# A decoder layer whose expert stage begins the loads of its gates from ScalarE instead of SyncE

## The reference

```python
def block(xb):                                   # 128 tokens, 1024 features
    q = (xb @ w_query).reshape(tb, 8, 2, 128)
    s = jnp.einsum('thpc,hpnc->thpn', q, sub_keys)
    top_s, top_i = lax.top_k(s, 16)
    ...                                          # 16 x 16 candidates a head, the best 16 are kept
    g = jax.nn.softmax(best_s, axis=-1)
    u = expert_u[idx]                            # idx: 8 heads x 16 of 16384 experts
    h = jax.nn.gelu(jnp.einsum('thkd,td->thk', u, xb), approximate=False)
    w = (g * h).astype(xb.dtype)
    return jnp.einsum('thk,thkd->td', w, expert_v[idx])
```

## Time and profile before

| | |
|---|---|
| time, median of 3 runs | 2946.75 us (2942.84 to 2950.31) |
| the profiled execution | 2942.5 us, of which the span in the profile is 2940.7 us |
| PE busy | 2642.6 us (90%) |
| DVE busy | 2408.1 us (82%) |
| ACT busy | 867.9 us (30%) |
| POOL busy | 1319.5 us (45%) |
| moved by DMA | 685.24 MB, 233 GB/s over the span |
| the expert phase | from about 1207 us to the end |

### The profile page before, as it was taken

How to read it: one execution, slowest core, us unless ns; L and a number is a source line. 1 busy time by engine, 2 the same in 40 slices (tenths; PEclk the granted TensorE clock), 3 DMA queues, 4 the chain that set the end, 5 groups by cost and what they waited for, 6 DMA issues and landing times. The chain is left out here.

```text
span 2940.7 us, 46951 instructions
## 1 busy us (share of the span) xinstructions
PE 2642.6 (90%) x17459; PEld 1721.0 (59%) x17459; DVE 2408.1 (82%) x4501; ACT 867.9 (30%) x1463; POOL 1319.5 (45%) x869
## 2 busy tenths in 40 slices
PE   8999888798867765699999999999999999999996
PEld 3566655458867764455555555555555555555552
DVE  3244555574999998489999999999999999999998
ACT  2333333211114555422222222222222222222223
POOL 2110000210014442046666666666677767766772
PEclk9999989799978885799999999999999999999998
DMA  4000010261002243789999999999999999999994
GB/s 155 23 15 15 15 72 15 88 250 51 1 1 115 114 163 150 287 293 354 359 351 357 364 347 361 362 353 368 324 339 347 346 344 348 332 354 339 340 337 170
DMA packets 262958, 685.24 MB, mean 233 GB/s; under 512 B 35624, under 2 KB 118184, under 8 KB 258352
## 3 DMA queue, kind: packets, MB, share of 16 engines
q0 software_dynamic: 110592, 402.70, 36.8%
q1 hardware_dynamic: 152240, 280.98, 27.4%
HBM read 624.89 MB, written 58.72 MB: 232 GB/s over the span
## 5 line engine op out<-in xcount | busy, mean ns | idle before, releaser
L1886 PE MATMUL h_psum<-early 128*128 128x384 bf16 (+1 forms) x6144 | 859.2, 300 | 23.4 <-issue 12.7
L1904 PE MATMUL o_psum<-v_split,w_split 128*128 128x512 bf16 x3840 | 856.7, 381 | 20.1 <-DVE wide L1745 20.0
L1886 PEld LDWEIGHTS h_psum<-early 128*128 128x128 bf16 x6144 | 602.6, 98 | 279.4 <-issue 26.6
L1904 PEld LDWEIGHTS o_psum<-v_split,w_split 128*128 128x128 bf16 x3840 | 375.5, 98 | 461.4 <-DVE wide L1745 25.3
L1701 POOL DMA_INDIRECT early<-v_blocks,pick_index x320 | 486.2, 1520 | 200.7 <-DVE wide L1757 119.1
L1701 POOL DMA_INDIRECT early<-u_rows,pick_index x320 | 426.4, 1333 | 329.5 <-DVE dots L1753 214.8
L1757 DVE SCALAR_TENSOR_TENSOR wide<-early,dots,wide 128x1024 f32<-128x1024 f32 x320 | 399.4, 1281 | 34.0 <-DMA early<-v_blocks,pick_index 33.3
L1753 DVE CUSTOM_DVE_ANT_0 early<-early,wide 128x1024 f32<-128x1024 f32 x320 | 380.7, 1220 | 25.5 <-DMA early<-u_rows,pick_index 24.6
L1648 ACT ACTIVATE w_split<-act_out 128x640 bf16<-128x640 f32 x128 | 94.3, 737 | 706.1 <-DVE act_out L1721 648.4
L1635 ACT ACTIVATE act_out<-h_psum 128x384 f32<-128x384 f32 (+1 forms) x256 | 97.2, 431 | 522.5 <-PE h_psum L1886 479.7
L1110 PE MATMUL r_t_psum<-rt_x_t,early 128*128 128x128 f32 (+1 forms) x1920 | 234.6, 283 | 0.0
(11 more groups left out here) (202 smaller groups left out, 2961.2 us busy)
## 6 DMA issues: line engine op xcount, KB each, us to landing
early<-u_blocks SPq DMA_DIRECT2D x128, 512.0 KB
early<-v_blocks SPq DMA_DIRECT2D x128, 512.0 KB
gates<-wide SPq DMA_DIRECT2D x20, 2048.0 KB, 6.3
gate<-gates SPq DMA_DIRECT2D x32, 1280.0 KB
early<-w_query SPq DMA_DIRECT2D x8, 1024.0 KB, 5.9
att_w_raw<-w_fox SPq DMA_DIRECT2D x4, 1536.0 KB, 7.0
early<-u_rows,pick_index POOLq DMA_INDIRECT x320
early<-v_blocks,pick_index POOLq DMA_INDIRECT x320
```

Of the source, the lines that this page charges most:

```text
L1886: mm = pe.matmul(h_psum[k][:, half, 0:width * P], u_split[:, k, part, c], xs[:, first:first + width, xpart, c, :], start=(c == 0 and part ...
L1904: mm = pe.matmul(o_psum[(DENSE * p + t) % 2][:, half * 512:half * 512 + 512], w_split[:, p, q, part, t * P:(t + 1) * P], v_split[:, p, q, ...
```

## The change

SP no longer waits for `w_done` and no longer begins the loads of the gates inside `refill`. ACT begins them, behind `split_w_hi` of the fourth block of a group. That call has already waited for `gated` of the same block, so the buffer has been read for the last time; no other wait is added. The loads of groups 0 and 1 stay with SP. The 30 transfers have the same source, target and size. They now belong to ACT's DMA queue, which nothing used before.

```diff
@@ refill, on SP
                         if not (end and j >= 2 * GROUP - 2):
                             sp.wait_ge(v_split_done, b + 1)
                             load_v(b + 2, j % 2)
-                        if j % GROUP == GROUP - 1 and not end:
-                            sp.wait_ge(w_done, b + 1)
-                            load_gate(2 * i + 2 + j // GROUP, j // GROUP)
@@ blocks_of, on ACT
                         split_w_hi(b, j)
+                        if j % GROUP == GROUP - 1 and not (isinstance(i, int) and i == last):
+                            g, p = 2 * i + 2 + j // GROUP, j // GROUP
+                            act.dma_start(gate[:, p], gates[:, :, bass.ds(g * GROUP, GROUP), :]).then_inc(gate_in[p], 16)
```

## The result

The changed kernel took 2974.88 us in the median, the kernel before 2946.94. These are medians of eight executions each; one of the eight of either kernel was disturbed (4622.56 and 8551.71 us) and is left out of the ratio, which goes by the means of the other seven, 2971.77 and 2946.43. The ratio is 1.0086, with a 95% interval of 1.0061 to 1.0111. The forecast was 2933. The profiled execution took 2975.9 us, 33.4 us more than that of before.

The account below looks back on a forecast made before the run. PE was taken to bound the early expert groups and DVE, waiting for gathers, the later ones. 2942.5 - 13.8 + 0 + 0 = 2928.7 us, 2932.9 against the median, forecast 2933; 8-in-10 range 2921 to 2952.

Parts of the forecast that it names:

- the early half: Expert phase, 12 groups from 1407.38 to 2032.95 us, mostly dot products with U rows; PE bounds it, no gain expected.
- the later one: Expert phase, 14 groups from 2032.95 to 2784.68 us, mostly additions of V rows; DVE bounds it at 53.70 us a group.
- the 22 given as the most that could be gained: Later 14 groups: at 1.57 us less a group PE bounds them too, so the gain stops at 22 us.
- PE's pace of 52.13 us a group: Group time in the 12 early groups, where PE is always busy; taken as the floor for the later groups.
- ACT's 30 loads: Gate loads newly issued by ACT: up to 7 us each covered by ACT's idle time, so cost 0; uncovered, 17 us.
- The rule that another issuing engine gives no bandwidth: Objection from the skill: all transfers share 16 DMA engines; by it alone gain 0, time 2947.
- the load begins earlier: Gate load moves 4.8 us earlier, ahead of U and V, into supposed DMA slack; the 13.8 us gain rests on it.
- the 6 us at 0.91 and 320 GB/s: DMA window from 2457.27 to 2463.27 after DVE's passes without takes, said to carry 0.46 MB of gates for nothing.
- cost nothing: U and V landing some 4 us later behind the gates: 20 us and more of slack before their readers.
- The expected 1.0 us less of waiting a group: DVE's gather waits in the later 14 groups: a third of 2.96 us goes away, giving 13.8 us.
- the expected 52.7: Group time in us forecast for the 14 later groups, down from 53.70 and still over PE's 52.13.
- The rival that said slower: Three DMA queues with equal turns crowd out gathers: 9 us later half, 8 us early, 2955 to 2964; chance 0.17.

Follow-up runs that it names:

- e3: Kernel before with the 30 gate loads of the loop left out, output not valid: 0.9899 of before, 2918.7 us.
- e4: Kernel before with SP's gate load moved behind the V load of the next group's second block: 0.9902 of before, 2920.95 us.
- e2: Changed kernel with ACT's gate load made to wait for `w_done`, about where SP began it before: 1.0000 of before.
- e1: Kernel before with SP's gate load moved ahead of the U and V loads of the fourth block, still in SP's queue: 1.0082 of before.
- e6: Kernel before with SP's gate load straight behind V of the fourth block, waiting for `gated` instead of `w_done`: 0.9989 of before.
- e14: As e4, but the gate load stands behind the V load of the next group's first block: 0.9908 of before.
- e5: As e4, but SP's gate load stands ahead of U and V in that second block, behind a wait for `gated`: 0.9996 of before.
- e15: Changed kernel with ACT's gate load moved to the second block of the next group, ahead of U and V: 0.9993 of before.
- e8: Changed kernel with SP holding the fourth block's U and V loads until `w_done`: 1.0128 of before.
- e13: As e4, with SP also holding U and V of the fourth block until the low part is made: 0.9913 of before.
- e7: Changed kernel with each gate load as one 10 KB run a partition instead of 20 runs of 512 bytes: 1.0065 of before.
- e12: Kernel before with each gate load as one 10 KB run a partition instead of 20 runs of 512 bytes: 1.0046 of before.

## Why the prediction was wrong

**What held.** In the kernel before, PE never stands in the early half, and DVE's waits for gathers bound the later one. Without gate loads PE waits for nothing and the time falls by 1.0% (e3). That is some 30 us, more than the 22 given as the most that could be gained: the limit took PE's pace of 52.13 us a group from the early half, and in e4 the 14 groups from the gate load of 2066.27 to that of 2790.24 take 51.7 each. ACT's 30 loads cost nothing that shows (e2). The rule that another issuing engine gives no bandwidth (the Trainium skill, DMA: Bandwidth & Descriptors, section "Issuing engines are not separate DMA queues") held as well: by either queue the time is the same in the same place, 1.0082 (e1) and 1.0086 ahead of U and V, 1.0000 (e2 and before) behind them.

**The step that failed** is "the load begins earlier", with the gain built on it. It took the 6 us at 0.91 and 320 GB/s for free room, 0.46 MB of it, by the 396 GB/s that gathers reach. The gates are slower: 0.53 MB in 89.6% of 2 us, about 296 GB/s, in the window from 2415 to 2417. An estimate by that rate and by the share of time that was free, 0.09 of 6 us, is 0.16 MB of the 1.31. With the gates in that place the engines carried no more than before. And it asked only whether U and V, pushed back by the gates, would be late for their readers. They were not. But it put their move at "cost nothing" without asking what it does to the gathers, and what the gates do to the gathers begun beside them. Before, 0.81 MB of U and V had gone 6 us behind U's issue; now 0.54 MB of them run more than 5 us behind it, where DVE takes again. And the gather begun beside the gate load gets no packet for 4 us in the group shown. The expected 1.0 us less of waiting a group came out as (59.0 - 41.5) / 14 = 1.25 us more, and the group takes 55.00 us instead of the expected 52.7. The early half, which was to stay as it was, is 8.6 us longer.

**What the runs show in its place.** The place of the load has two parts of about 0.9% each, which add up in the cells that were measured:

| | behind V | ahead of U and V |
|---|---|---|
| 4th block, two `down` tiles | 1.0000 (before), 0.9989 (e6) | 1.0086 (changed), 1.0082 (e1) |
| 1st or 2nd block, one `down` tile | 0.9908 (e14), 0.9902 (e4) | 0.9996 (e5), 0.9993 (e15) |

The prediction moved the load the wrong way along the second part and left the first, which had the gain, as it was. It had read both halves of this in the profile: ten takes close together, and the load in that stretch.

**The rival that said slower** named 2955 to 2964, and the gathers begun at the start of the dense takes as the victims. The victims are nearly right: those that wait longest are begun beside the gate load, some 3 us ahead of the first of these takes. Its 8 us for the early half fit the 8.6 measured; its 9 us for the later half were 18.3. Its mechanism, a third queue with equal turns, is not needed, since one queue is as slow (e1). Nor does the trace show equal turns: with three queues at work the gathers have no packet from 2154 to 2158 and 48.5% of the engines from 2158 to 2163.

**What stays open.** In the trace, the gates in the pause leave a gather without a packet for 4 us, and then U and V share the engines with it. Which of the two makes the 0.9% was not taken apart; e8 moves U and V but leaves the gates beside them. The gather's own share is not the same everywhere: e1 is as slow with few long waits. U and V held back cost 0.1% when gates are not near (e13) and 0.4% on top of gates that are ahead (e8 against the changed kernel), so the two do not simply add. In six of the 12 long waits POOL's instruction for the late gather lasts 3.9 to 4.2 us, and in the other six 1.9 to 2.0 us, with waits of up to 5.4 us. So the long instruction is not needed for a long wait. Whether it adds to it, and where it comes from, was not tried.

## What to carry to other kernels

A prefetch with a whole group of slack still has a price where its bytes meet a stream that someone waits for. Place it by the density of that stream: here the same 30 loads cost next to nothing in a thin stretch, 1.0% in a dense one and 1.9% ahead of other loads in a dense one. Before filling a gap in DMA traffic, ask which load stands in it now and where that one goes; and test a new queue and a new moment apart, since one edit often changes both.

## What had not been expected of the hardware

The run length changes how a load shares the engines with gathers. In the changed kernel from 2163 to 2168, 12 us and more behind its issue at 2151.36, the gates, in runs of 512 bytes, moved 0.15 MB beside gathers of 4 KB rows:

```profile
q0 software_dynamic: 483, 1.76, 86.9%
q10 hardware_dynamic: 301, 0.15, 10.3%
q1 hardware_dynamic: 18, 0.06, 3.0%
```

In e7, where a gate load is issued at 2152.54, the same window has no gates left. Its 10 KB runs moved 0.67 MB from 2156 to 2158, with 10.7% of the engines for gathers:

```profile
q10 hardware_dynamic: 65, 0.67, 79.7%
q0 software_dynamic: 22, 0.09, 10.7%
```

This fits the 0.46% that 10 KB runs cost behind V (e12): the load takes more from the gathers while both have work. That this is the reason was not tested.

SP can be held by its own queue. In e4 the U load that follows the gates held SP for 3.78 us instead of 0.33, at no cost that shows (e4 has no wait of ACT for a U or V block); in e1 and e5, where U follows within 1.2 us, it is 4 to 7 us in most groups, and ACT does wait. The row of e4:

```profile
2430.16 0.55 SPq L1585 DMA_DIRECT2D gate<-gates  x1
2440.01 3.78 SPq L1508 DMA_DIRECT2D early<-u_blocks  x1
```

POOL's gather instruction, mostly 0.94 to 2.0 us, was 3.9 to 4.2 us in 16 of 768 cases in the changed kernel and in 10 before, all of them gathers of rows of V. No run here shows why.
